# Groups of unread one-pass products behind the first 32 modulation rows of a two-block transformer kernel

## The reference

```
c_act = silu(c)
mod = c_act @ ada_w + ada_b            # (2048) @ (2048 x 6*2048)
sh1, sc1, g1, sh2, sc2, g2 = split(mod, 6)
h = rms_norm(x, mix_pre_g) * (1 + sc1) + sh1
y = hybrid_mixer(h, ...)               # attention and a causal convolution, then w_out
x = x + g1 * rms_norm(y, mix_post_g)
h = rms_norm(x, ffn_pre_g) * (1 + sc2) + sh2
x = x + g2 * rms_norm(swiglu_ffn(h, w_gate, w_up, w_down), ffn_post_g)
```

## Time and profile before

| | us |
|---|---|
| device time, median of 2 runs | 2616.21 (2616.01 to 2616.41) |
| span of the profiled execution | 2614.0 |
| device time less span | 2.2 |
| TensorE busy | 2567.3 (98%) |
| VectorE busy | 1691.6 (65%) |
| ScalarE busy | 1222.0 (47%) |
| first row's product starts | 12.52 |
| first projection product starts | 100.90 |

### The profile page before, as it was taken

How to read it: one execution, slowest core, us unless ns; L and a number is a source line. 1 busy time by engine, 2 the same in 40 slices (tenths; PEclk the granted TensorE clock), 3 DMA queues, 4 the chain that set the end, 5 groups by cost and what they waited for, 6 DMA issues and landing times.

```text
span 2614.0 us, 54085 instructions
## 1 busy us (share of the span) xinstructions
PE 2567.3 (98%) x21414; PEld 2438.5 (93%) x21414; DVE 1691.6 (65%) x2347; ACT 1222.0 (47%) x1667; POOL 49.9 (2%) x98
## 2 busy tenths in 40 slices
PE   5999999999999999999999999999999999999999
PEld 1488889999999999999999999999999999999999
DVE  1388867686666666557655655554766776666667
ACT  1343455554444444446545444444544444444445
POOL 0000000000000000000000000000000000000000
PEclk9899999999999999999999999999999999999999
DMA  9988868466666666554544455555455555555554
GB/s 390 383 322 306 289 210 311 168 204 226 224 226 225 226 224 209 183 192 161 170 145 139 151 176 179 188 178 187 151 187 186 188 187 185 187 186 188 186 186 138
DMA packets 136065, 545.53 MB, mean 209 GB/s; under 512 B 15121, under 2 KB 15377, under 8 KB 123537
## 3 DMA queue, kind: packets, MB, share of 16 engines
q1 hardware_dynamic: 126288, 474.08, 54.1%
q0 software_dynamic: 9216, 67.11, 7.2%
q10 hardware_dynamic: 448, 2.75, 0.3%
HBM read 541.78 MB, written 2.10 MB: 208 GB/s over the span
## 4 chain that ended last, share of the span: by engine, by line
PE 94%; DMA 2%; DVE 2%; ACT 1%; issue 0%; ACTq 0%; DVEq 0%; SPq 0%
PE bank L1797 20%; PE bank L1799 20%; PE bank L1798 20%; PE bank L1943 9%; PE bank L1945 9%; PE bank L1944 9%; PE bank L1833 2%; DMA ada_pre<-in_ada_w 2%; PE bank L1883 1%; PE bank L1854 1%; DVE w_lo L1086 1%; ACT w_hi L540 1%; DMA bf<-in_f_bias 1%; PE bank L1901 1%; PE bank L1893 0%
## 5 line engine op out<-in xcount | busy, mean ns | idle before, releaser
L1086 DVE TENSOR_TENSOR w_lo<-raw,w_hi 128x1024 fp32r<-128x1024 f32 x836 | 1014.5, 1224 | 655.3 <-ACT w_hi L540 654.3
L540 ACT ACTIVATE w_hi<-raw 128x1024 fp32r<-128x1024 f32 x836 | 875.1, 1058 | 869.8 <-PE bank L1799 502.2
L1797 PE MATMUL bank<-h_hi,w_hi 128*128 128x258 f32 (+2 forms) x2832 | 803.4, 284 | 2.4 <-DVE tg L1400 0.8
L1798 PE MATMUL bank<-h_lo,w_hi 128*128 128x258 f32 (+2 forms) x2832 | 797.7, 282 | 0.0
L1799 PE MATMUL bank<-h_hi,w_lo 128*128 128x258 f32 (+2 forms) x2832 | 797.6, 282 | 0.0
L1797 PEld LDWEIGHTS bank<-h_hi,w_hi 128*128 128x128 f32 x2832 | 533.0, 188 | 19.0 <-issue 16.5
L1798 PEld LDWEIGHTS bank<-h_lo,w_hi 128*128 128x128 f32 x2832 | 533.1, 188 | 0.8 <-issue 0.7
L1799 PEld LDWEIGHTS bank<-h_hi,w_lo 128*128 128x128 f32 x2832 | 533.0, 188 | 0.0
L1943 PE MATMUL bank<-hid_hi,w_hi 128*128 128x256 f32 x1280 | 353.9, 276 | 0.0
L1944 PE MATMUL bank<-hid_lo,w_hi 128*128 128x256 f32 x1280 | 353.6, 276 | 0.0
L1945 PE MATMUL bank<-hid_hi,w_lo 128*128 128x256 f32 x1280 | 353.6, 276 | 0.0
(11 more groups left out here) (263 smaller groups left out, 3094.8 us busy)
## 6 DMA issues: line engine op xcount, KB each, us to landing
raw<-in_w_in SPq DMA_DIRECT2D x208, 512.0 KB, 4.3
raw<-in_w_ffn_up SPq DMA_DIRECT2D x176, 512.0 KB, 4.3
ada_raw<-in_ada_w POOLq DMA_DIRECT2D x64, 1024.0 KB, 7.1
raw<-in_w_gate SPq DMA_DIRECT2D x88, 512.0 KB, 4.2
raw<-in_w_up SPq DMA_DIRECT2D x88, 512.0 KB, 3.5
raw<-in_w_down SPq DMA_DIRECT2D x88, 512.0 KB, 4.1
raw<-in_w_ffn_down SPq DMA_DIRECT2D x88, 512.0 KB, 4.4
ada_pre<-in_ada_w SPq DMA_DIRECT2D x32, 1024.0 KB, 8.5
```

Source lines behind the costliest of these rows:

```text
L540: act.activation(w_hi[:, slot], raw[:, slot], ACT.Copy).then_inc(hi_ready, 1)
L1086: dve.tensor_tensor(w_lo[:, slot], raw[:, slot], fp(w_hi[:, slot]), ALU.subtract).then_inc(lo_ready, 1)
L1797: pe.matmul(dst, wh, x_hi(kt), start=first and k == 0, stop=False)
L1798: pe.matmul(dst, wh, x_lo(kt), start=False, stop=False)
```

## The change

A tile trial of 7168 fp32r elements a partition is laid over the first 28672 bytes of region r2, which nothing else uses in this stretch (sq lies from byte 28672 on). GpSimd fills it with 0.5 as its first instruction, and TensorE waits for that (trial_ready) before its first row. Behind the row's products of each of the 32 rows, and ahead of the channel sum or keep_busy, TensorE runs one group of products out of trial into banks 0 and 1 in turn, each with start and stop set. Nobody reads them, and the first projection starts these banks anew. A group is 12 products (9 for width 384, 7 for 512, and a pair group of 8 of 512 and 256 columns in turn). Each group has a width of its own, a byte offset modulo 256 of the moving operand and of the weights, and for two groups another first column in the bank.

```
--- before.py
+++ after.py
@@ -231,6 +231,7 @@
         rel_lo = place("rel_lo", "r3", 24608 + 4 * QSUM, [HEADS, QSUM], f32r)
         ga_s = place("ga_s", "r3", 20480, [128, 2, LIVE])
         gp_s = place("gp_s", "r3", 20480 + 2064, [128, 2, LIVE])
+        trial = place("trial", "r2", 0, [128, 7168], f32r)
         pcol = sb("pcol", [128, 7, 128])
         cwt = sb("cwt", [128, AT, CONV_K])
         ident = sb("ident", [128, 128])
@@ -272,6 +273,7 @@
         c_loaded, rows_loaded = sem("c_loaded"), sem("rows_loaded")
         consts = sem("consts")
         cact_ready = sem("cact_ready")
+        trial_ready = sem("trial_ready")
         pre_loaded = [sem(f"pre_loaded{n}") for n in range(4)]
         pre_used = sem("pre_used")
         ada_loaded = [sem(f"ada_loaded{n}") for n in range(ADA_RING)]
@@ -463,6 +465,7 @@
 
         @block.gpsimd
         def _(gp):
+            gp.memset(fp(trial[:, :]), 0.5).then_inc(trial_ready, 1)
             gp.memset(ident[:, :], 0.0).then_inc(consts, 1)
             gp.memset(ones[:, :], 1.0).then_inc(consts, 1)
             gp.memset(eps[:, 0:1], 1e-6).then_inc(consts, 1)
@@ -1854,12 +1857,45 @@
                     pe.matmul(bank[:, B_V, :], ident[:, :], pcol[:, 3:7, :].rearrange("p a n -> p (a n)"),
                               start=True, stop=True)
 
+            off = (-(base + region["r2"]) % 256) // 4
+
+            def unread(width, moving=192, weights=0, to=0, step=0, count=12):
+
+                for m in range(count):
+                    w0 = off + weights // 4 + 128 * (m % 4)
+                    m0 = off + 1024 + moving // 4 + step * (m % 4)
+                    pe.matmul(bank[:, m % 2, to:to + width], trial[:, w0:w0 + 128], trial[:, m0:m0 + width],
+                              start=True, stop=True)
+
+            def unread_pair(moving=192, low=192, weights=0):
+
+                for m in range(8):
+                    w0 = off + weights // 4 + 128 * (m % 4)
+                    m0 = off + 1024 + moving // 4
+                    width = 256 if m % 2 else 512
+                    pe.matmul(bank[:, m // 2 % 2, 0:width], trial[:, w0:w0 + 128], trial[:, m0:m0 + width],
+                              start=True, stop=True)
+
+            TRIALS = [(unread, (254, 64, 128)), (unread, (240, 64, 128)), (unread, (192, 64, 128)),
+                      (unread, (128, 64, 128)), (unread, (256, 32, 128)), (unread, (256, 64, 128)),
+                      (unread, (256, 0, 128)), (unread, (256, 128, 128)), (unread, (256, 192, 128)),
+                      (unread, (256, 64, 0)), (unread, (256, 64, 64)), (unread, (256, 64, 192)),
+                      (unread, (256, 0, 0)), (unread, (258, 120, 128)), (unread, (258, 248, 128)),
+                      (unread, (258, 64, 128)), (unread, (258, 0, 128)), (unread, (258, 192, 128)),
+                      (unread, (258, 56, 128)), (unread, (258, 184, 128)), (unread, (260, 112, 128)),
+                      (unread, (264, 64, 128)), (unread, (272, 64, 128)), (unread, (272, 0, 128)),
+                      (unread, (320, 64, 128)), (unread, (384, 64, 128, 0, 0, 9)), (unread, (512, 64, 128, 0, 0, 7)),
+                      (unread, (512, 0, 128, 0, 0, 7)), (unread_pair, (64, 64, 128)), (unread, (258, 120, 128, 254)),
+                      (unread, (258, 120, 128, 128)), (unread, (258, 120, 0))]
+            pe.wait_ge(trial_ready, 1)
             pe.wait_ge(consts, 5)
             pe.wait_ge(cact_ready, 1)
             for n, b in enumerate((B_S, B_P)):
                 for kt in range(KT):
                     pe.wait_ge(pre_loaded[kt % 4], 16 * (4 * n + kt // 4 + 1))
                     ada_products(ada_pre, kt % 4, kt, b).then_inc(pre_used, 1)
+                    form, args = TRIALS[KT * n + kt]
+                    form(*args)
                     if n == 0:
                         channel_sum(kt, SEQ)
                     elif kt >= KT - 5:
```

## The result

The changed kernel takes 2636.68 us (median of 2 runs, 2635.99 to 2637.36) against 2616.21: a ratio of 1.0077, 95% interval 1.0047 to 1.0106. That is 20.5 us more where 19.2 was forecast. Its profiled execution spans 2635.6 us, 21.6 more than before.

What follows compares the result with a forecast made beforehand. TensorE bounds from 101 us on, DMA mostly before; with the groups TensorE paces the rows. Row, group and change costs put the first projection product at 120.1 us, 19.2 later: 2616.2 + 19.2 = 2635.4 us, range 2625 to 2650.

Steps and rivals of the forecast that it cites:

- wait ahead of turn_rows: Before the first turn_rows: ScalarE copies the sum row under the last group and channel sum, so the 2.4 us wait goes.
- row 16 and its group: First row of the second sixteen: row at 1.19 us plus a group of width 258 at 1.43 us.
- rows 17 to 26: Second sixteen, rows without keep_busy: TensorE needs 2.68 us a row, 0.2 above the DMA's 2.48.
- rows 27 to 30: Rows with keep_busy: 2.05 us each, 0.2 us each for changes, plus their groups, 14.8 us together.
- row 31 to the first product: Tail before the first projection: the former 7.16 us all moves along, and the last group adds 1.43 + 0.2 us.
- The memset and trial_ready: Start of GpSimd's work and TensorE's new wait: at most 7.0 us, costing nothing, with 3.8 us of cover.
- Rival B: Rows 16 to 26 take 2.48 us each, paced by DMA, if changes cost nothing: shift 13.0 us, 2629 us; chance 0.12.
- changes between kinds: On TensorE between a row's products and its group: two changes cost 0.2 us a row, ends 0 and 0.4.
- The price of products in the ratio of width 256: TensorE's unread products: 0.443 ns a column, 0.142 us at width 320, 0.227 at 512, 0.085 at 192.
- Rival C: Offsets or widths add 6 to 18 us, or a low clock until 23 us adds about 2: 2641 to 2653; chance 0.13.
- Rival D: Unread products cost as fp32 ones do, 0.315 us per 256 columns: 73 us more, 2708 us; chance 0.05.
- Rival E: All added products hidden, each row with its group under 2.48 us, or the change misruns: 2616 us; chance 0.02.

Runs made afterwards that it cites:

- none: Changed kernel with all 32 groups left out, memset of trial and its wait kept: ratio 1.0002 to the kernel before, first projection product at 102.6 us.
- double: Changed kernel with each group run twice: ratio 1.0249 to the kernel before, first projection product at 166.7 us.
- first16: Changed kernel with only the groups behind rows 0 to 15: ratio 1.0035 to the kernel before, first projection product at 108.9 us.
- last16: Changed kernel with only the groups behind rows 16 to 31: ratio 1.0041 to the kernel before, first projection product at 112.3 us.
- copy_first: Changed kernel with ScalarE copying the first sixteen rows' sums before the root: ratio 1.0059 to the kernel before, first projection product at 116.6 us.
- gap_filled: Changed kernel with two keep_busy products ahead of the first turn_rows: ratio 1.0070 to the kernel before, first projection product at 119.4 us.
- half: Changed kernel with every group at half its count: ratio 1.0016 to the kernel before, first projection product at 105.9 us.
- half_copy_first: Changed kernel with groups at half count and ScalarE's copy ahead of the root: ratio 1.0006 to the kernel before, first projection product at 102.4 us.

## Why the prediction was right, and which terms were off

| step | forecast | measured |
|---|---|---|
| row 1 starts | 18.8 | 18.40 |
| last channel sum of the first sixteen ends | 66.0 | 63.9 |
| wait ahead of turn_rows | 0 | 2.4 |
| turn_rows | 0.98 | 1.80 |
| row 16 and its group | 2.6 | 4.74 |
| rows 17 to 26 | 26.9 | 27.1 |
| rows 27 to 30 | 14.8 | 14.1 |
| row 31 to the first product | 8.8 | 8.6 |
| first product | 120.1 | 122.7 |

- The memset and trial_ready cost nothing: shown by none. The memset took 6.07 us; the bound was 7.0.
- TensorE paces all rows: shown by the waits, by double, and by first16 and last16. Rival B (DMA takes over in the second sixteen) is out: rows were 2.62 us and more apart. It needed changes between kinds that cost nothing; the first step of a group is 0.22 us where the others are 0.12, and the step from a group to a row 0.21, together the 0.2 that the sum had.
- The price of products in the ratio of width 256 held for wide ones: 320, 384 and 512 took 0.147, 0.173 and 0.234 us a step against 0.142, 0.170 and 0.227. For narrow ones it failed: 0.112 at width 128 and 192 against 0.08 and 0.085, worth 0.7 us.
- Rival C (dear offsets) is out: at width 256 all offsets lie between 0.115 and 0.120, at 258 between 0.119 and 0.122. Width 258 at offset 0 ran at the lower clock in the changed kernel; in copy_first and gap_filled it ran at full clock and took 0.120 and 0.121. The lower clock up to 23 us did not come either: row 1 ran at full clock from 18.40 us on.
- Rival D is out: doubling costs 44 us for 367 products, 0.12 each. Rival E (all hidden) is out by the ratio.
- The changes between kinds were priced 0.2 us a row. In the first sixteen they cost less, as the channel sum shortens from 0.63 to 0.53 us behind a group, 1.5 us over fifteen rows; this is most of the 2.1 us by which these rows came early.
- The step that was wrong in this sum: "ScalarE copies the sum row under the last group and channel sum (its 2.4 us wait goes)". What is queued ahead of the copy on ScalarE was not looked at. The wait stayed, and the clock fell behind it: 2.7 and 3.0 us by copy_first and gap_filled. Cheaper early rows and rows 27 to 30 took back half, which is why the total was off by only 1.3 us in the medians and 2.4 in the traces. That closeness is in part luck. Where the wait does go and the clock stays up, as the sum had it, the first product came at 116.6 (copy_first), 3.5 us ahead of the 120.1 of the forecast: the missed wait and its lower clock hid that the other terms were too dear.

## What to carry to other kernels

Filler work on an engine that waits for transfers is free only up to the transfer's own period, here 2.48 us a row: with the copy ahead of the root half the products cost 1.5 us and all of them 15.7. Before a wait is said to vanish, read what stands ahead of the releasing instruction in its engine's queue. A short wait of TensorE can cost more than its length, as the next products may run at half clock, and where they free the slots of a transfer ring and the transfers set the pace, the transfers lose the time for good (half: 3.5 us more than half_copy_first).

## What the runs showed of the hardware

A stream of one-pass products has two floors, the moving columns (0.113 us at 256) and the weight columns (0.112 us at 128, 0.058 at 64); with 128 weight columns the second one decides below 256 moving columns, with 64 it does at 64 but no longer at 128 (0.060). A change from a product in full float32 to a one-pass one or back adds about 0.1 us to a step (0.22 and 0.21 against 0.12). The lower clock followed a gap of 2.4 us in seven of nine profiled executions, for lengths that differ by execution: row 16 and its group took 4.74 and 3.97 us in two executions of the same kernel, and 2.63 where there was no gap.
